# Low parts of the weights on Pool: four subtractions of 256 columns in place of one of 1024

## What is computed

```
def swiglu(h, w_gate, w_up, w_down):
    return (jax.nn.silu(h @ w_gate) * (h @ w_up)) @ w_down

q, k, v, z, xbc, dt_raw, g_lru, x_lru = split_cols(h @ w_in)
...
x = x + jnp.concatenate([att, ssd, lru], axis=-1) @ w_out
x = x + swiglu(rmsnorm(x, norm_ffn), w_gate, w_up, w_down)
...
for l in range(DEPTH_2):
    y = swiglu_2(rms_norm(x, ffn1_pre_g[l]), ffn1_w_gate[l], ffn1_w_up[l], ffn1_w_down[l])
    ...
    y = hybrid_mixer(rms_norm(x, mix_pre_g[l]), w_in[l], ...)
    ...
    y = memory_xattn(rms_norm(x, xa_pre_g[l]), rms_norm(mem, xa_mem_g[l]), ...)
```

## Time and profile before

| | |
|---|---|
| median of 3 runs | 3493.95 us (3493.79 to 3502.77) |
| the profiled execution | 3493.52 us, of which 3492.2 us span |
| granted TensorE clock, mean | 0.984 |
| PE busy | 3348.5 us, 96% |
| DVE busy | 1385.1 us, 40% |
| ACT busy | 1224.4 us, 35% |
| Pool busy | 1275.6 us, 37% |
| HBM traffic | 81 GB/s over the span |

### The profile page before, as it was taken

One profiled execution on the slowest core, in us unless ns is written; L12 is line 12 of the kernel. 1 busy time (PEld: TensorE's weight loads), 2 busy tenths in 40 slices (PEclk: granted clock), 3 DMA queues, 4 the chain that ended last, 5 costly groups with the idle time before them and its releaser, 6 DMA issues.

```text
span 3492.2 us, 42040 instructions
## 1 busy us (share of the span) xinstructions
PE 3348.5 (96%) x16296; PEld 2708.0 (78%) x16296; DVE 1385.1 (40%) x2531; ACT 1224.4 (35%) x2245; POOL 1275.6 (37%) x569
## 2 busy tenths in 40 slices
PE   5989999999999999999999999999989999999997
PEld 4866688887888777877778887888777877678886
DVE  4574543205330524654353304431334563544311
ACT  4443332223222343453332223322333444433221
POOL 3322244443444342233234443444352233234442
PEclk9999999999999999999999999999999999999998
DMA  3211123332222231122123322322231112123321
GB/s 127 80 49 59 50 87 98 100 99 76 97 94 100 85 113 48 47 70 71 62 80 98 98 95 80 98 98 97 86 128 49 42 64 88 49 67 102 98 95 63
DMA packets 79109, 287.05 MB, mean 82 GB/s; under 512 B 8896, under 2 KB 9152, under 8 KB 78400
## 3 DMA queue, kind: packets, MB, share of 16 engines
q1 hardware_dynamic: 77616, 278.42, 24.3%
q10 hardware_dynamic: 1296, 5.94, 0.4%
HBM read 282.23 MB, written 2.10 MB: 81 GB/s over the span
## 4 chain that ended last, share of the span: by engine, by line
PE 82%; DVE 8%; ACT 3%; POOL 3%; issue 3%; DMA 0%; ACTq 0%; POOLq 0%; DVEq 0%
PE bank L251 24%; PE bank L253 23%; PE bank L252 23%; PE bank L933 4%; PE bank L957 3%; POOL wlo L246 2%; PE bank L944 2%; DVE hlo L620 1%; ACT hhi L668 1%; DVE x L615 1%; ACT whi L234 1%; PE bank L2651 1%; DVE m_xbc L1544 1%; DVE m_V L2308 1%; PE bank L551 1%
## 5 line engine op out<-in xcount | busy, mean ns | idle before, releaser
L246 POOL TENSOR_TENSOR wlo<-raw,whi 128x1024 fp32r<-128x1024 f32 (+1 forms) x520 | 1230.6, 2367 | 1995.3 <-ACT whi L234 1960.1
L251 PE MATMUL bank<-hhi,whi 128*128 128x512 f32 x2416 | 965.9, 400 | 20.5 <-POOL wlo L246 10.2
L252 PE MATMUL bank<-hlo,whi 128*128 128x512 f32 x2456 | 959.0, 390 | 0.0
L253 PE MATMUL bank<-hhi,wlo 128*128 128x512 f32 x2416 | 944.3, 391 | 0.0
L234 ACT ACTIVATE whi<-raw 128x1024 fp32r<-128x1024 f32 (+1 forms) x536 | 533.9, 1034 | 378.4 <-PE bank L253 362.9
L251 PEld LDWEIGHTS bank<-hhi,whi 128*128 128x128 f32 x2416 | 455.8, 189 | 127.0 <-issue 32.0
L252 PEld LDWEIGHTS bank<-hlo,whi 128*128 128x128 f32 x2456 | 463.5, 189 | 91.8 <-issue 1.8
L253 PEld LDWEIGHTS bank<-hhi,wlo 128*128 128x128 f32 x2416 | 455.0, 188 | 97.1
L251 PE MATMUL bank<-ff_ahi,whi 128*128 128x512 f32 x880 | 342.8, 390 | 0.0
L253 PE MATMUL bank<-ff_ahi,wlo 128*128 128x512 f32 x880 | 342.4, 389 | 0.0
L252 PE MATMUL bank<-ff_alo,whi 128*128 128x512 f32 x840 | 326.8, 389 | 0.0
(11 more groups left out here) (346 smaller groups left out, 4367.2 us busy)
## 6 DMA issues: line engine op xcount, KB each, us to landing
raw<-wstream SPq DMA_DIRECT2D x516, 512.0 KB, 3.7
raw<-wstream SPq DMA_DIRECT2D x20, 256.0 KB, 3.1
x<-xT ACTq DMA_DIRECT2D x4, 512.0 KB, 13.0
xa_v<-memT ACTq DMA_DIRECT2D x2, 1024.0 KB, 4.8
outT<-x SPq DMA_DIRECT2D x1, 2048.0 KB, 6.2
consts<-consts ACTq DMA_DIRECT2D x1, 1103.0 KB, 9.6
m_lw<-lru_w ACTq DMA_DIRECT2D x1, 544.0 KB, 3.3
par<-par SPq DMA_DIRECT2D x2, 248.0 KB, 14.1
```

The costliest lines, as they stand in the source:

```text
L246: g.tensor_tensor(h.lo[:, 0:h.cols], h.raw[:, 0:h.cols], h.hi[:, 0:h.cols].bitcast(F32), ALU.subtract).then_inc(h.lo_made.sem)
L251: t.matmul(out, l[0], r[0], start=start, stop=False)
L252: t.matmul(out, l[0], r[1], start=False, stop=False)
L253: return t.matmul(out, l[1], r[0], start=False, stop=stop)
```

## The change

`weight_lo` on Pool issues the subtraction in pieces of `PIECE = 256` columns. Only the last piece raises `lo_made`; there is no wait between the pieces of a half. Where DVE makes the low part (`e` given), it stays one instruction. Line numbers move by 1 up to the edit and by 4 behind it; the subtraction of L246 is L249 there.

```
@@ -18,6 +18,7 @@
 HALF = 1024
+PIECE = 256
 SLOTS = 4
...
@@ -243,7 +244,10 @@
         g.wait_ge(*h.hi_made[0])
         if h.n > 0:
             g.wait_ge(*k.halves[h.n - 1].lo_made[0])
-        g.tensor_tensor(h.lo[:, 0:h.cols], h.raw[:, 0:h.cols], h.hi[:, 0:h.cols].bitcast(F32), ALU.subtract).then_inc(h.lo_made.sem)
+        step = h.cols if e else PIECE
+        for o in range(0, h.cols, step):
+            last = g.tensor_tensor(h.lo[:, o:o + step], h.raw[:, o:o + step], h.hi[:, o:o + step].bitcast(F32), ALU.subtract)
+        last.then_inc(h.lo_made.sem)
```

## The result

| | before | after |
|---|---|---|
| median of 20 runs each | 3496.83 us (3492.53 to 3507.22) | 3504.58 us (3502.32 to 3510.93) |
| ratio | | 1.0021 [1.0014, 1.0027] |
| the profiled execution | 3493.52 us, span 3492.2 | 3505.39 us, span 3503.9 |

The changed kernel is 7.75 us slower. That is inside the range, and under the 0.3% from which two medians can be told apart as the text of the prediction counts it; the forecast was +4.0. Twenty executions of each do tell it: the interval excludes 1. The forecast of 3498 us stood on a median of three executions, 3493.95; the twenty of before have 3496.83, so 2.9 of the 6.6 us between 3498 and 3504.58 are the base and 3.75 the change.

What follows compares the result with a forecast made beforehand. It took PE as the bound (busy 3348.5 of 3492.2 us), Pool mattering only where PE waits for it or DVE is held up. 13.5 + 1.5 - 11.0 = +4.0 on 3493.95 gave 3498 us, range 3484 to 3517.

Steps and rivals of the forecast that it cites:

- The fixed part: On Pool, 0.18 us per piece independent of size: a piece takes 0.73 us, each half 0.45 us more.
- the exposed halves: Halves PE waits for at the start, in entries and compression: 26 halves pay 0.45 us each in full, 11.7 us.
- the mixers: Convolutions, recurrence, attention, retention: 11.0 us of gains against 1.5 for convolutions and 1.8 ahead of two powers, -7.7 us.
- the feed-forward parts: Feed-forward stages: nothing booked, as PE has no wait for Pool there; a late stretched half would prove the forecast wrong.
- The compression stage: Twelve halves in a row, once in each of two layers; PE waits up to the seventh, 3.15 us each.
- The dense places: Convolutions, L644 and L2308, where two-input DVE instructions follow one another: blocked time stays the same, about no gain.
- rival B: Everywhere beside Pool, each DVE wait falls to a quarter, dense stretches included: -20 us, 3474 us; chance 0.10.
- Pool hands over between pieces: Where DVE is blocked, Pool lets it in after each piece, which holds it about 0.55 us, not 2.1.
- Rival A: Pool does not let DVE in between queued pieces, so gains go to zero: 3509 to 3519 us; chance 0.26.
- The gains: DVE blocked for less: 2.9 us at L1632 and L1634, 4.8 at L2522 in two layers, 3.3 elsewhere; 11.0 us.
- The convolutions: First block: pieces alternate with DVE, a half takes about 5.2 us, and a late column tile costs 1.5 us.
- The likeliest case: Whole kernel: the forecast itself, +4.0 us to 3498 us, its own range 3490 to 3506, chance 0.50.

Runs made afterwards that it cites:

- e2: Changed kernel with pieces of 256 only in both blocks' mixers and the convolutions, one instruction elsewhere: 3489.72 us against 3497.74 for the kernel before.
- e6: Changed kernel with pieces of 256 only in the first block's recurrence and attention and beside the second's attention, retention and memory: 3487.66 us against 3499.05 before.
- e5: Changed kernel with the two halves at the start of each feed-forward's second pair left as one instruction each: 3498.98 us against 3497.74 before.
- e3_ff: Changed kernel with pieces only in feed-forward stages, down projections and attention to the memory, not right behind a power: 3510.78 us against 3497.74 before.
- b_again: The kernel before, unchanged, run once more for a second profile: 3493.0 us.
- e1_waited: Changed kernel with pieces of 256 only at the start, right behind each entry's power and in the compression stages: 3508.2 us against 3497.74 before.
- e3_again: The kernel with pieces in the feed-forward stages alone, unchanged, executed again for a second profile: 3511.9 us.
- e4_512: Changed kernel with two pieces of 512 columns in place of four of 256, in all stages: 3494.18 us against 3499.05 before.
- e8_chosen_512: Pieces of 512 in place of 256, only in the chosen mixer stages, without convolutions and output projection: 3486.58 us against 3498.22 before.
- e7_128: Changed kernel with pieces of 128 columns, eight to a half, in all stages: 3541.25 us against 3498.22 before.

## Why the prediction was right or wrong

**The fixed part and the exposed halves: right.** A piece takes 0.739 us (forecast 0.73); a half costs 0.42 us more where somebody waits (0.45). The start lost 1.8 us (1.8). All eight entries wait 1.32 us (forecast 1.35, had 0.90); one of them:

```profile
1200.47 2.80 POOL L249 TENSOR_TENSOR wlo<-raw,whi 128x256 fp32r<-128x256 f32 x4
...
1203.41 0.47 PE L255 MATMUL bank<-hhi,whi 128*128 128x512 f32 x1 [1.32 <-POOL wlo L249]
```

The power at the attention's end comes 0.84 us later (2 x 0.45). The 102 cycles of the Trainium skill (GPSIMD Engine Reference, section "Performance pitfalls for Q7 kernels") gave an estimate of 0.26 us a half, which is too low here: 0.42 was measured.

**The three parts.** The terms of the sum can be set beside the experiments that ran them alone: the exposed halves 11.7 booked, 10.5 measured; the mixers -7.7 booked, -8.0 measured; the feed-forward parts nothing booked, +13.0 measured (9.7 at equal clock, 5.7 in PE's idle time). Two of the three were sized well, and the third is the step that failed.

**The compression stage: right in kind, slightly low.** Inside the stage PE lost 3.5 us in layer 1 (drift from +0.98 at its first wait to +4.49), not 3.15, because it waits for ten halves and not for seven: the growing delay used up the slack that the eighth to the tenth had. But its first wait ended 1.5 us earlier against the work around it than before (3.96 us in the earlier trace rows, 2.46 after), since L2308 did gain something.

**The dense places: booked at no gain, nearly right for L644, too low for L2308.** DVE's four L2308 take 3.76 us and 3.54 in place of 7.91 and 2.30 (7.30 against 10.21 for the eight), and seven additions of L644 take 6.87 us, not the 7.5 forecast nor the 6.0 of rival B. A piece blocks for 0.41 us (forecast 0.55), and the blocked time did not fall to a quarter:

```profile
L2312 DVE TENSOR_TENSOR m_V<-m_U,par x16: 635/1044/1065, 1210.2 to 2562.0; 128x256 f32<-128x256 f32 x16
```

The median of 16 is the blocked length, 1044 against 635 ns: twelve of them are held up by about 0.41 us and two by 0.22. Before, six were, by 1.5 to 2.1 us. So the blocked time of the sixteen fell from 11 to 5 us, by half; the prediction had it unchanged, rival B at a quarter.

**Pool hands over between pieces: right.** Rival A would have left the scan at 3.27 us and the longest L2522 at 2.5 or more; they are 1.64 and 0.83. The overlap of 0.03 us, which spoke for A, goes together with strict turns. The sentence of the Trainium skill (GPSIMD Engine Reference, section "Instruction dispatch") that a Pool instruction does not wait for all cores to finish the one before may hold, and the port is passed on all the same: it would have made A likelier, and the trace went the other way.

**The gains: right in place, each somewhat small.** At 209.18 of before 3.1 us came back (2.9), 0.9 more up to 210.84, and 2.4 at 155 and 181; from 96 to 298 the drift fell by 7.5 us, of which the kernel before against itself shows 1.6. The scaling of L2522 gave 2.7 us at 1508.35 and the same in layer 2 (2.4). What the step missed is what stands behind it. The window there, before and after:

```profile
1508.00:1514.00 6.00, 5.46 (x24) 0.72 0.28 91
```

```profile
1511.00:1517.00 6.00, 5.52 (x35) 1.00 0.55 176
```

Without the 3.04 us wait of the earlier trace rows the clock stays at 2.4 GHz, which gave another 1.5 us up to 1514, and 0.3 came at 1527.60. So a layer gained about 4.6 us here in this pair of traces, not 2.4. The experiments are more sober: -8.0 (e2) and -11.4 (e6), with the terms for convolutions and powers taken off, leave 12 to 13 us of gains in all, against 11.0 booked.

**The convolutions: mis-sized.** The step said that two halves of 5.2 us would make one product later by what its tile can spare, and booked 1.5. Measured: eight pieces took 8.9 us in place of 5.4, PE's wait grew by 1.5 us, and the half clock behind it, which the step did not know, added 1.7 before 1.0 was given back at 96.14: 2.2 net. The 1.5 came at the wait for the low part itself; the step had it at a product that uses the late tile, so the equal number is luck.

**The feed-forward parts: the step that failed.** The working booked nothing for them because PE has no wait for Pool there before, and put "a stretched half turns up late" only among the ways to be wrong. By e5 the two halves at the start of each second pair are 6.5 us, nearly the whole result and more than the miss of 3.75. The rows to see it were there: a half ends 0.16 us ahead of its product, with DVE instructions of two inputs beside it. Having no wait is not having slack; and the rule of the turns that was used for the convolutions was not applied to a second place of the same make.

**The likeliest case came in**, then, with errors of both signs. Between the two profiled executions, 11.7 us apart, the traces show some 20 us of gains (7.5 in the first block, 4.6 in each layer behind the compression, 1.5 ahead of it in each) against 11.0 booked. Costs were larger by 6.5 in the second pairs, 0.7 in the convolutions, 0.7 in the compression stages, and by stretches at half clock at 389 to 399 and at 2680 (times of after), some 7 us. That the sum came within 3.75 us of the median is partly luck: a missing cost of 10 us or so stands in it against other errors.

**Still open.** The three parts alone sum to +10.5 - 8.0 + 13.0 = +15.5 us, all together cost 7.75. A part of this is the clock: e3_ff ran at a mean granted clock of 0.981, the changed kernel at 0.9835. At equal clock the parts sum to +12 and the whole is +8.6, and by PE's idle time it is +3.7 and +4.2 (last section). What is left between these was not settled, nor why the time at half clock is so long when only the feed-forward parts are in pieces.

## What to carry to other kernels

Splitting an instruction helps only where another engine is blocked by it on the path that sets the end, and no one waits for the split instruction itself: here the same edit was worth -11.5 us in chosen stages and +7.75 everywhere. Before splitting, look at the slack of each consumer, not at its waits: pieces that take turns with the other engine stretch the split work (2.5 to 3.7 us a half), and ten halves with 0.16 us of slack or so cost 6.5 us. With all stages split two pieces were better than four (-4.9 against +7.75), since each piece pays the fixed part. In the chosen stages the medians are alike, but in the profiles four gave PE twice as much idle time back as two. Compare kernels by many executions, and look at the clock of each before calling a few us the change's.

## What the runs showed of the hardware

**Turns between Pool and DVE.** Queued Pool instructions without a wait let a blocked DVE instruction in between, one each; it is held up for 0.41 to 0.55 us by a piece of 256 columns, 1.0 to 1.1 by one of 512. This agrees with the Trainium skill (SBUF — State Buffer, section "Who interferes with whom"), by which the lock of the shared pair of ports holds for one instruction; that the locked engine's own work grows in turn, from 2.5 to 3.7 us a half (4.4 in the convolutions), is the part that decided here.

**PE's clock is a second account.** For each profile I summed PE's idle time up to its last product, and PE's busy time while the granted clock was 1.2 GHz, from the records of the clock. What is left of the span after taking off the idle time and half of the latter is nearly the same in all:

| kernel | span | PE idle | busy at 1.2 GHz | span - idle - half of that |
|---|---|---|---|---|
| before | 3492.2 | 127.1 | 80.3 | 3324.9 |
| b_again | 3491.7 | 125.0 | 81.9 | 3325.8 |
| after | 3503.9 | 130.2 | 92.3 | 3327.5 |
| e1_waited | 3504.1 | 134.7 | 87.8 | 3325.5 |
| e2_beside | 3490.3 | 115.4 | 101.2 | 3324.4 |
| e3_ff | 3516.8 | 130.9 | 123.6 | 3324.2 |
| e3_again | 3510.6 | 132.6 | 105.4 | 3325.2 |
| e4_512 | 3493.1 | 123.7 | 84.8 | 3327.0 |
| e5_not_pair1 | 3499.2 | 126.2 | 95.8 | 3325.2 |
| e6_chosen | 3491.3 | 116.5 | 98.1 | 3325.7 |
| e8_chosen_512 | 3484.7 | 121.0 | 75.4 | 3326.0 |
| e7_128 | 3542.3 | 151.6 | 130.8 | 3325.3 |

The idle time repeats within 2 us for one kernel (127.1 and 125.0; 130.9 and 132.6) and adds up over the parts: against the mean of the two profiles of before, e1 has +8.7, e2 -10.7, e3 +5.7, together +3.7, and the changed kernel has +4.2. The time at half clock need not repeat (123.6 and 105.4 for e3) and does not add up.

It makes most of the spread among executions of one kernel. Each execution's mean granted clock is on record, to 0.001, for 54 of the kernel before (the sessions of e1, e4 and e7). Time and clock go together with a correlation of -0.93: 12 executions at 0.984 took 3492.4 to 3496.7 us, 11 at 0.981 took 3499.1 to 3504.1, the one at 0.979 3507.8. Within the kernels, 0.001 of clock goes with 2.2 us (2.5 for the kernel before alone). That fits the table: 0.001 of 3497 us is 7 us at half clock, PE is busy in three quarters of such time, and half of that is 2.6.

With these 2.2 us the runs can be compared at equal mean clock. The fourth column is an estimate from the means of 4 to 20 executions, good to 1 or 2 us; the twenty of before beside the changed kernel have no clock on record, so all 54 stand in for them:

| kernel | median less before | mean clock, before in its session | at equal clock | PE idle less 126.1 |
|---|---|---|---|---|
| after | +7.75 | 0.9835, 0.9824 (all 54) | +8.6 | +4.1 |
| e1_waited | +10.5 | 0.9826, 0.9826 | +10.5 | +8.6 |
| e2_beside | -8.0 | 0.9819, 0.9826 | -8.1 | -10.7 |
| e3_ff | +13.0 | 0.9808, 0.9826 | +9.7 | +5.7 |
| e5_not_pair1 | +1.2 | 0.9832, 0.9826 | +1.8 | +0.1 |
| e4_512 | -4.9 | 0.9839, 0.9823 | -1.3 | -2.4 |
| e6_chosen | -11.4 | 0.9826, 0.9823 | -10.4 | -9.6 |
| e8_chosen_512 | -11.6 | 0.9852, 0.9824 | -6.0 | -5.1 |
| e7_128 | +43 | 0.9755, 0.9824 | +26.7 | +25.5 |

The last two columns agree within 2 to 5 us, though the one comes from single profiles and the other from all executions. For e7 (0.972 to 0.977) and e8 (0.984 to 0.986) the clock of every execution lies at or beyond the edge of before's beside them (0.980 to 0.984), so there it is hardly chance: the kernel's own sequence of work has a part in it. No run here shows how.

The same stretch in two executions of the kernel before shows it, first the first profile, then b_again:

```profile
384.00:402.00 18.00, 15.12 (x80) 1.00 0.09 30
```

```profile
384.00:402.00 18.00, 15.20 (x67) 0.81 0.09 30
```

Same waits, same work, and one of them ran part of it at 1.2 GHz. In the profile after the clock is 0.72 in this stretch, which is most of the drift from -3.1 to +1.7 that the table above shows there; a single profile can't say that the change caused it. So of the 11.7 us between the two profiled spans only 3.1 are idle time of PE, 6.0 are half clock and 2.6 are left over; by the medians, the change costs 7.75.
